# Weighting two experts' rows by diagonal matrices on TensorE, with the next layer's head moved into the rounds loop

## The reference

```python
def rmsnorm(x, g):
    y = x * rsqrt(mean(x * x, axis=-1) + EPS)
    return y * g

for l in range(2):
    sh1, sc1, g1, sh2, sc2, g2 = ada_modulation(c, w_ada[l], b_ada[l])
    h = rmsnorm(x, norm1[l]) * (1 + sc1) + sh1
    x = x + g1 * mixing(h)          # one input projection, four mixers, one output projection
    h = rmsnorm(x, norm2[l]) * (1 + sc2) + sh2
    # 16 experts; each token's two best, with gates that sum to 1
    x = x + g2 * (gate_a * expert_a(h) + gate_b * expert_b(h))
y = rmsnorm(x, norm_f)
```

## Time and profile before

| | us |
|---|---|
| median of three executions | 1345.33 |
| lowest and highest | 1344.44 and 1346.76 |
| the profiled execution's own time | 1343.43 |
| its span in the trace | 1341.9 |
| PE busy, of the span | 1099.3 (82%) |
| DVE busy | 452.2 (34%) |
| ACT busy | 263.5 (20%) |
| POOL busy | 278.6 (21%) |

### The profile page before, as it was taken

The page is one execution under the profiler, slowest core; times in us unless marked ns, Lnnn a source line. Parts: engine busy times, 40 slices in busy tenths (PEclk is TensorE's granted clock), DMA queues, the critical chain, the costliest instruction groups (busy, mean ns, idle before and its releaser), DMA issues.

```text
span 1341.9 us, 12934 instructions
## 1 busy us (share of the span) xinstructions
PE 1099.3 (82%) x4154; PEld 577.7 (43%) x4154; DVE 452.2 (34%) x1053; ACT 263.5 (20%) x592; POOL 278.6 (21%) x372
## 2 busy tenths in 40 slices
PE   3799999879996199999539999988999609999950
PEld 0355655545442044444215565554544304444420
DVE  0211222656224133333261112255712322333327
ACT  0221111446000011111132102133610101111113
POOL 1451000531121300000274200034101230000023
PEclk7799999999998599999859999999999759999985
DMA  9956110773205769999664832057300556999935
GB/s 324 348 200 243 64 49 32 266 291 118 94 0 160 317 231 360 369 370 367 253 219 139 308 101 78 32 194 268 119 0 0 211 195 220 360 366 370 368 145 206
DMA packets 61393, 280.35 MB, mean 209 GB/s; under 512 B 9264, under 2 KB 10416, under 8 KB 45472
## 3 DMA queue, kind: packets, MB, share of 16 engines
q1 hardware_dynamic: 31184, 183.00, 37.4%
q0 software_dynamic: 27856, 93.68, 19.2%
q10 hardware_dynamic: 2304, 3.04, 0.6%
HBM read 230.88 MB, written 51.21 MB: 210 GB/s over the span
## 4 chain that ended last, share of the span: by engine, by line
PE 78%; DMA 6%; DVE 5%; issue 5%; POOL 3%; SPq 1%; ACT 1%; POOLq 0%; DVEq 0%; ACTq 0%
PE ps L1257 17%; PE ps L1180 10%; PE ps L929 10%; PE ps L1276 8%; PE ps L983 5%; PE ps L976 5%; PE ps L930 3%; PE ps L1157 3%; PE ps L1246 2%; DMA arena<-in_w_n 2%; PE ps L938 2%; PE ps L1127 2%; PE ps L1137 2%; DMA expert_in<-arena,pos_i 1%; POOL expert_in L857 1%
## 5 line engine op out<-in xcount | busy, mean ns | idle before, releaser
L1257 PE MATMUL ps<-arena 128*128 128x512 f32 x512 | 229.8, 602 | 3.5 <-DVE arena L1895 3.5
L929 PE MATMUL ps<-arena 128*128 128x512 f32 x320 | 163.8, 593 | 0.0
L1257 PEld LDWEIGHTS ps<-arena 128*128 128x128 f32 x512 | 98.7, 193 | 128.0 <-issue 123.2
L1180 PE MATMUL ps<-arena 128*128 128x512 f32 x320 | 138.8, 593 | 2.7 <-issue 2.7
L1276 PE MATMUL ps<-arena 128*128 128x512 f32 x256 | 115.4, 594 | 3.4 <-issue 3.4
L1895 DVE COPY arena<-ps 128x512 f32<-128x512 f32 x32 | 22.1, 692 | 262.6 <-PE ps L1246 262.6
L930 PEld LDWEIGHTS ps<-arena 128*128 128x128 f32 x320 | 60.8, 190 | 76.5 <-issue 76.5
L1180 PEld LDWEIGHTS ps<-arena 128*128 128x128 f32 x320 | 60.2, 190 | 77.1 <-issue 77.1
L883 POOL DMA_DIRECT2D expert_out<-arena x32 | 17.1, 536 | 310.3 <-DVE arena L1916 299.7
L1246 PE MATMUL ps<-arena 128*128 128x128 f32 x256 | 35.0, 282 | 49.8 <-DMA arena<-expert_in 49.8
L983 PE MATMUL ps<-arena 128*128 128x512 f32 x160 | 70.3, 592 | 0.0
(11 more groups left out here) (255 smaller groups left out, 1409.4 us busy)
## 6 DMA issues: line engine op xcount, KB each, us to landing
arena<-in_w SPq DMA_DIRECT2D x96, 1024.0 KB, 8.8
arena<-in_w_ada SPq DMA_DIRECT2D x48, 1024.0 KB, 6.8
expert_out<-arena POOLq DMA_DIRECT2D x33, 512.0 KB, 7.7
expert_in<-arena POOLq DMA_DIRECT2D x2, 8192.0 KB, 24.6
arena<-expert_in POOLq DMA_DIRECT2D x32, 512.0 KB, 7.7
arena<-in_w_t SPq DMA_DIRECT2D x10, 1024.0 KB, 8.9
arena<-in_w_out SPq DMA_DIRECT2D x8, 1024.0 KB, 6.0
arena<-mod_rows POOLq DMA_DIRECT2D x16, 512.0 KB, 8.3
```

What stands on the lines that cost most here:

```text
L929: mm(out[:, 0:N_LAT], lhsT, rhs_of[:, 0:N_LAT], start=(k == 0), stop=(k == n - 1))
L1180: ins = mm(out[:, n * 512:(n + 1) * 512], yT[:, k, t * P:(t + 1) * P], w[k // 2][:, k % 2, n * 512:(n + 1) * 512], start=(k == 0), stop=(k ...
L1257: ins = mm(out, hsT[b][:, k, :], w[:, k, :], start=(k == 0), stop=(k == KD - 1))
```

## The change

**Combine.** When a layer's routing is done, ACT writes ten 128x128 matrices `gate_diag`, each with one tile's gates on its diagonal. In the loop PE computes for a tile `gate_diag[a] @ y_a` for both experts into two PSUM banks (`combine`, four calls of 128x512), DVE multiplies the sum by the modulation row straight out of PSUM and adds to `x`. In layer 0 that holds for tiles 0 to 2, while tiles 3 and 4 keep the old way, now on ACT as `weighted`. In layer 1 it holds for all five. `COMBINE_AT` names the banks; tile 3 waits until tile 0 was read, tile 4 until tile 1 was.

**Head.** The mean squares, the roots (POOL, behind the ten gathers), the normalised rows (ACT in layer 0's loop, DVE at the start of the program) and the columns of tile 0 (`first_columns`) move into the body of the loop. After them PE goes on with `narrow_low(0)` of layer 1 once tiles 0 to 2 were read from PSUM and the columns are copied, and with `columns_of(1)` once all five tiles were read.

**End.** `norm_f` is loaded before layer 1's experts. DVE forms an output row inside the loop, one tile behind the update, and SP instead of ACT writes it out. `y_1st` moves to other places in SBUF.

```diff
+COMBINE_AT = [4, 0, 2, 4, 0]
-        y_1st = view(at_h, TT, D)
-        normf_row = view(at_c + D, D)
+        normf_row = view(at_a, D)
+        y_1st = [view(at_d + 2 * D + t * D, D) for t in range(TL)] + [view(at_a + SLOT, D)]
+        gate_diag = view(at_a + SLOT + D, 2 * TT, P)
...
+                if l + 1 == DEPTH:
+                    filled(sp, l, ("mlO", 1, 0))
+                    sp.dma_start(normf_row, A["norm_f"].broadcast_to((P, D))).then_inc(normf_in, 16)
-            wait(sp, x_done, sp.snap(turns, min_val=2, max_val=10) * TT + (TT + 1))
-            sp.dma_start(normf_row, A["norm_f"].broadcast_to((P, D))).then_inc(normf_in, 16)
+            for t in range(TT):
+                wait(sp, y_final, sp.snap(turns, min_val=2, max_val=10) * TT + (t + 1))
+                sp.dma_start(O["y"][t * P:(t + 1) * P, :], h2[:, t, :]).then_inc(y_out, 16)
...
@@ POOL, in the loop behind the ten gathers
+                        for t in range(TT):
+                            head_inverse_root(pool.snap(turns, min_val=0, max_val=10) * TT + (TT + t + 1), t)
...
@@ PE
                 def columns_of(t):
                     out = acquire(pe, l, ("hT", t))
+                    if l and t == 1:
+                        pe.wait_ge(combine_read, pe.snap(turns, min_val=1, max_val=10) * TT + CREDIT)
...
+                def first_columns(l, turn):
+                    out = place(l, ("hT", 0))
+                    pe.wait_ge(head_rows, turn * TT + 1)
+                    for k in range(KD):
+                        ins = tr(out[:, k * P:(k + 1) * P], xn[:, 0, k * P:(k + 1) * P], ident)
+                    ins.then_inc(head_columns, 1)
...
+                pe.wait_ge(head_copied, pe.snap(turns, min_val=0, max_val=10) * 2 + 2)
...
+                def combine(base, turn, t):
+                    pe.wait_ge(yg_in[t], base * 2 + 32)
+                    if t >= 3:
+                        pe.wait_ge(combine_read, turn * TT + (CREDIT + t - 2))
+                    lo = COMBINE_AT[t] * BANK
+                    for a, y_a in enumerate((y_1st[t], y_2nd[:, t, :])):
+                        for n in range(2):
+                            ins = mm(ps[:, lo + n * BANK:lo + (n + 1) * BANK], gate_diag[:, a * TT + t, :],
+                                     y_a[:, n * BANK:(n + 1) * BANK], start=(a == 0), stop=(a == 1), skip_group_check=True)
+                    ins.then_inc(combine_full, 1)
...
+                        for t in range(3):
+                            combine(base, turn, t)
+                        if l + 1 < DEPTH:
+                            first_columns(l + 1, turn + 1)
+                        else:
+                            for t in range(3, TT):
+                                combine(base, turn, t)
...
@@ ACT
+                    if l + 1 < DEPTH:
+                        act.wait_ge(ahead_used.sem, ahead_used.at(l, KD))
+                    for a in range(2):
+                        for t in range(TT):
+                            ins = act.activation(gate_diag[:, a * TT + t, :], ident, ACT.Copy, scale=gates[:, a, t:t + 1])
+                    ins.then_inc(diag_ready.sem, 1)
...
+                        def updated(t):
+                            act.wait_ge(x_done, turn * TT + (TT + t + 2))
+                            head_square(turn * TT + (TT + t), t)
+                        def normalised(t):
+                            act.wait_ge(head_root, turn * TT + (TT + t + 1))
+                            act.activation(xn[:, t, :], x[:, t, :], ACT.Copy, scale=rstd[:, 0, t:t + 1]).then_inc(head_rows, 1)
...
+                        updated(0)
+                        if l + 1 < DEPTH:
+                            weighted(3)
+                            normalised(0)
+                            weighted(4)
+                            first_columns(l + 1, turn + 2)
+                            updated(1)
+                            for t in range(2, TT):
+                                updated(t)
+                                normalised(t - 1)
+                            normalised(TT - 1)
+                        else:
+                            for t in range(1, TT):
+                                updated(t)
...
@@ DVE, update(t) for tiles 0 to 2 of layer 0 and all of layer 1
+                                dve.wait_ge(combine_full, turn * TT + (t + 1))
+                                V(y_t, ps[:, lo:lo + D], rows[:, 0, t // TL, :], ALU.mult).then_inc(combine_read, 1)
...
+                            dve.wait_ge(combine_read, turn * TT + (CREDIT + t + 1))
                             V(x[:, t, :], x[:, t, :], y_t, ALU.add).then_inc(x_done, 1)
+                        update(0)
+                        update(1)
+                        if l + 1 < DEPTH:
+                            update(2)
+                            first_columns(l + 1, turn + 2)
+                            update(3)
+                            update(4)
...
+                        else:
+                            dve.wait_ge(normf_in, 16)
+                            last_row(turn * TT + (TT + 1), 0)
+                            for t in range(2, TT):
+                                update(t)
+                                last_row(turn * TT + (TT + t), t - 1)
+                            last_row(turn * TT + 2 * TT, TT - 1)
```

More of the change, by code:

```diff
@@ L451, in mixer_kernel @@
         gate2_in = per_layer("gate2_in", 16 * 2)
-        squares = per_layer("squares", TT)
-        root_x, root_q, root_kv, root_mixed = (per_layer(n, TT) for n in ("root_x", "root_q", "root_kv", "root_mixed"))
+        head_squares, head_eps, head_root, head_rows = (sem(f"head_{n}") for n in ("squares", "eps", "root", "rows"))
+        head_columns, head_copied = sem("head_columns"), sem("head_copied")
+        root_q, root_kv, root_mixed = (per_layer(n, TT) for n in ("root_q", "root_kv", "root_mixed"))
         eps_added = sem("eps_added")
-        xn_ready = per_layer("xn_ready", TT)
         q_zeroed = per_layer("q_zeroed", 1)
@@ L739, in _ @@
             modulation_inputs(0)
+            for t in range(TT):
+                head_inverse_root(t + 1, t)
             for l in range(DEPTH):
                 ada_bias = A["b_ada_q"][bass.ds(l, 1)].rearrange("a j (g n) -> (a j) g n", n=512)
-                for t in range(TT):
-                    wait(pool, squares.sem, squares.at(l, t + 1))
-                    inverse_root(l * 4 * TT + t + 1, 0, t, root_x.sem)
                 wait(pool, x_done, pool.snap(turns, min_val=0, max_val=10) * TT + (TT + 1))
@@ L908, in _ @@
                 rounds()
-            for t in range(TT):
-                pool.wait_ge(squares.sem, squares.at(DEPTH, t + 1))
-                inverse_root(DEPTH * 4 * TT + t + 1, 0, t, root_x.sem)
         @block.tensor
@@ L1321, in _, with head_square, first_columns @@
             act.reg_mov(turns, 0)
-            def mean_square(n, t):
-                if n is not None:
-                    act.wait_ge(squares.sem, n)
+            def head_square(n, t):
+                act.wait_ge(head_squares, n) if n is not None else None
                 act.activation(junk, x[:, t, :], ACT.Square, scale=D ** -0.5,
-                               accum_out=stat[:, 0, t:t + 1]).then_inc(squares.sem, 1)
+                               accum_out=stat[:, 0, t:t + 1]).then_inc(head_squares, 1)
+            def first_columns(l, n):
+                act.wait_ge(head_columns, n)
+                out = place(l, ("hT", 0))
+                for k in range(4, KD):
+                    ins = act.activation(hT[:, k, 0:P], out[:, k * P:(k + 1) * P], ACT.Identity,
+                                         scale=mod_a[:, 0, k:k + 1], bias=mod_s[:, 0, k:k + 1])
+                ins.then_inc(head_copied, 1)
             for t in range(TT):
-                mean_square(t or None, t)
+                head_square(t or None, t)
             for l in range(DEPTH):
@@ L1532, in _ @@
                 rounds()
-                updates = act.snap(turns, min_val=1, max_val=10) * TT
-                for t in range(TT):
-                    act.wait_ge(x_done, updates + (t + 2))
-                    mean_square(squares.at(l + 1, t), t)
-            for t in range(TT):
-                act.wait_ge(y_final, t + 1)
-                act.dma_start(O["y"][t * P:(t + 1) * P, :], h2[:, t, :]).then_inc(y_out, 16)
         @block.vector
@@ L1559, in _, with head_row, last_row, first_columns @@
             dve.sem_inc(x_done, TT + 1)
+            dve.sem_inc(y_final, TT)
             links = [0]
+            def head_row(n, t):
+                dve.wait_ge(head_root, n)
+                dve.tensor_scalar(xn[:, t, :], x[:, t, :], rstd[:, 0, t:t + 1], None, ALU.mult).then_inc(head_rows, 1)
+            def last_row(n, t):
+                dve.wait_ge(head_root, n)
+                dve.scalar_tensor_tensor(out=h2[:, t, :], in0=x[:, t, :], scalar=rstd[:, 0, t:t + 1], in1=normf_row,
```

(8 more changed lines are left out.)

83 lines of the change are left out of this document (53 added, 30 removed).

## The result

The changed kernel took 1334.95 us (median of four, 1332.42 to 1335.77), the kernel before beside it 1345.03 (four, 1344.44 to 1346.76): ratio 0.992 with an interval of 0.9903 to 0.9937, a gain of 10.1 us by the medians. The forecast gain of 12.9 would be a ratio of 0.9904, inside the second interval and just inside the first.

The account below looks back on a forecast made before the run. Three quarters of the span hang on TensorE, so gains come only where the chain leaves it: 10.7 between the layers plus 2.2 at the end, 12.9 us, from the 1345.33 median to 1332.4; range 1329 to 1338.5.

Parts of the forecast that it names:

- The step that carries the sum: Between the layers: `narrow_low(0)` starts at 686.85 instead of 696.04, and VectorE reaches tile 4's product by 693.1.
- steps 1 to 4: Between the layers: three combines, VectorE's updates, tile 0's root, row, transposes and column copies, ending with `narrow_low(0)` at 686.85.
- the second half of step 4: Between the layers: `narrow_low(0)` starts at 686.85 and, warm, takes 5.59 instead of 7.8, over at 692.4.
- the rival: Between the layers: clock falls again before `narrow_low(0)`, which takes 7.8; 1.6 us lost, total 1334.0; chance 0.12.
- The price of a cold combine: Both places: four calls take 3.44 us at full clock, plus a cold start of 2.5 once per place.
- ScalarE's margin: Between the layers: ScalarE has tile 1's columns at 700.3, 0.6 us before TensorE wants them at 700.9.
- ScalarE is late: Between the layers: TensorE waits 1 to 3 us at `narrow_low(1)`; total 1334 to 1336; chance 0.16.
- The end: End of the program: last output row over at 1335.3 against 1337.47, gain 2.2 us.
- What moves with it: Elsewhere: later bias table and `w_t` chunk, ten diagonal copies (at most 3.8 us) and `norm_f` load cost nothing.
- later loads eat the gain: Whole program: moved loads cancel the gain, time stays within a few us of 1345; chance 0.03.
- isn't what it says: Loop: added waits might hold it back, about 1345 us; chance 0.02.
- half clock throughout: Both places: every combine takes 6.88 us; net 9 us slower, 1354; chance 0.05 (the slower end).

Follow-up runs that it names:

- second interval: The changed kernel run again unaltered, against the kernel before: 1333.7 us, ratio 0.9907 [0.9894, 0.9921].
- idle calls: Changed kernel plus matmuls nobody reads, ahead of both layers' combines and of layer 1's `narrow_low(0)`: 1329.5 us; with only the latter set: 1330.49 us.
- roots off GpSimd: Changed kernel with layer 1's five closing roots taken by ScalarE (square root) and VectorE (reciprocal): 1332.03 us, ratio 0.9902.
- both mends again: Second run of the changed kernel plus unread matmuls in both places and layer 1's closing roots on ScalarE and VectorE: 1324.82 us, ratio 0.9851.
- layer 0 without TensorE weights: Changed kernel with unread matmuls and closing roots on ScalarE and VectorE, but layer 0's five tiles weighted by ScalarE and VectorE: 1326.21 us, ratio 0.985.

## Why the prediction was right, and where its terms were off

- **The step that carries the sum held.** `narrow_low(0)` was put at 686.85 - 657.53 = 29.3 after the copy and started at 29.3; tile 4's product was put at 35.6 and was over at 34.9. ScalarE, VectorE and TensorE follow in the order that steps 1 to 4 say.
- **The failed step is the second half of step 4**, "so `narrow_low(0)` starts at 686.85 instead of 696.04 and, warm, takes 5.59". It took 7.4, as the rival had it (7.8); `narrow_high(0)` started at 37.5 instead of 36.5, and the idle calls give 1.8 back. I had put 0.12 on that rival because a gap of 4.2 (it became 4.5) lay just under the 4.7 and 5.3 read off windows without any matmul. But the fall seen there came in quite a different stretch, and two readings of one fall each bound nothing. In the changed kernel itself the clock is down 2.5 us after the last expert's last matmul, which is over at 658.5:

```profile
658.00:661.00 3.00, 0.49 (x2) 0.00 (x0) 0.69 (x1) 0.60 (x1) 0.53 (x1) 0.98 0.18 74
661.00:664.00 3.00, 0.00 (x0) 0.00 (x0) 0.00 (x0) 0.00 (x0) 0.00 (x0) 0.50 0.42 175
```

  And around the gap of 4.5 us it fell in all three profiles that had the gap unfilled. The Trainium skill, "TensorE: Matmul & The Clock Gate", section "Why this matters for your kernels", warns of such gaps, and here the trace agrees: 7.4 us against 5.7.
- **The price of a cold combine** was put at 2.5 a place and measured 12.31 - 3 x 3.44 = 2.0 between the layers and 19.46 - 5 x 3.44 = 2.3 at the end. It is the same kind of loss as in the earlier trace rows.
- **ScalarE's margin** was put at 0.6 and was 3.4. Of the 2.8 more, 1.1 is the later start of `narrow_high(0)`, 0.7 that VectorE had `x` whole earlier than put (36.1 after the copy against 36.8), and 0.9 the last root: I priced the way from square to root at the 3.5 us of the earlier trace rows, and tile 0's took 2.3, its root 0.57 beside a product that VectorE reads from PSUM; tile 4's root, beside a copy out of PSUM, took 0.57 too. The rival "ScalarE is late" had no ground.

```profile
679.90 1.23 DVE L2075 TENSOR_TENSOR arena<-ps,arena 128x1024 f32<-128x1024 f32 x1 [0.95 <-PE ps L1319]
...
680.83 0.57 POOL L746 TENSOR_TENSOR arena<-arena 128x1 f32<-128x1 f32 x1 [0.18 <-POOL arena L744]
...
687.13 1.27 DVE L2079 SCALAR_TENSOR_TENSOR arena<-arena 128x1024 f32<-128x1024 f32 x1
687.35 1.48 POOL L746 TENSOR_TENSOR arena<-arena 128x1 f32<-128x1 f32 x1 [0.18 <-POOL arena L744]
```

The Trainium skill, "SBUF — State Buffer", section "Who interferes with whom", says that a VectorE operation with two inputs in SBUF and a GpSimd operation that reads SBUF get into each other's way, and that, outside its two-port modes, one with a single such input does not. These four rows agree with it, 0.57 against 1.48.
- **The end**: put at 2.2, the last row came 3.1 earlier, but the span only 1.9. The prediction took the end of the last output row for the end of the program and never priced GpSimd's closing drain, of which the kernel before has 4.5 us of slack (1337.15 against 1341.65). The output now lands 4.4 us earlier after the copy (3.1 from the row, 1.3 from the way to landing), while the last root, with which the drain starts, moved later: 36.2 after the copy against 33.5. The root was behind its tile's update before, too; but four output rows now stand between VectorE's updates, so that the last update is over at 34.4 instead of 31.6. Together that is 7 us, and the drain is 2.5 over. That the span's 1.9 lies so near the 2.2 is luck: the cheaper row and landing hide the drain. The roots off GpSimd give 2.6 back.
- **What moves with it** cost next to nothing, as put: beside the falls of the clock, only the sixteen experts of layer 1 took longer, 190.8 and 190.7 us in the two profiles of the changed kernel against 190.1 and 190.2 before; why wasn't looked for. The rivals "later loads eat the gain", "isn't what it says" and "half clock throughout" fell. For the last of them the prediction mistook lost time for time at half clock: half clock loses half of its time, so the low clock would have to last some 13 us longer in each place to eat the gain, not 6.5.
- **What the parts are worth** the prediction left out, for it needed only the sum. Its chain runs over TensorE's combines in both places; the runs show that, as the change stands, these bring nothing, that between the layers the order carries the gain, and that at the end the early load of `norm_f` carries most of it.

The point forecast is off by 1.3 to 2.5 us. By the stages the gain is 11.5 where 12.9 were put. Too much was put by the clock's 1.8 and the drain's 2.5, too little by tile 4's product (0.7 earlier), by the last row (0.9) and by the output's way to landing (1.3). The rest is chance, falls of some 1.7 each among it.

## What to carry to other kernels

When the work after a stage ends in a chain of equal steps (update, square, root, row), first weave the next stage's first tile in between: between the layers that was the gain here. At a program's end look first for a load that comes late. Moving arithmetic to an idle TensorE paid at the end, where it took work from VectorE (1.6 us cold, 3.0 warm, on the last row), and cost 0.6 warm and 1.5 to 2.4 cold between the layers, where it delays the first tile. A few matmuls without a reader kept the clock up in four of seven stretches ahead of the combines and in every gap ahead of `narrow_low(0)`; they were worth 1.8 and 2.1 us by the stages, 3 to 5 by the medians, and delayed nothing that was seen. And before pricing the last microseconds of a program, look at what each engine still has to close after its last instruction.

## What the runs showed that I had not expected

- GpSimd's closing drain took 7.15 to 8.1 us when tiny roots were its last work, and 15.9 to 17.1 when gathers were. Then it starts before the last of them are over: with both mends again from 1295.3 to 1311.8, with the last gather over at 1303.1; in the changed kernel from 1326.2, with the last root over at 1326.7. So it lasts some 9 us past the last gather (8.2 to 9.4) and 6.7 past the last root. With a root as the last work it ended the program in five kernels. What it waits for wasn't tried.
- A short fall to half clock in the attention stages comes and goes between executions of the same kernel, 1.6 to 1.8 us each, at a few places: here at 329 to 334 and 967 to 972 of the span, in others of these profiles at 284 to 289 (0.66, idle calls in both places) and 917 to 922 (0.66, layer 0 without TensorE weights).
- Idle calls with a gap of 1.6 to 2.1 us behind them left the first real matmuls at full clock in some executions and at half in others; without a gap (one profile) they were at full clock.
